# A two-block transformer layer on one core: first projection from the raw input, router logits from the unnormed residual

## What is computed

```python
def rmsnorm(x, g):
    return x * rsqrt(mean(x * x, axis=-1) + EPS) * g

h = rmsnorm(x, attn_pre_norm)                    # block 1
proj = h @ w_in
...
x = x + gt1 * (concat([att, conv]) @ w_out)      # block 2
h2 = rmsnorm(x, g_ffn) * (1 + sc2) + sh2         # modulate
aff = softmax(h2 @ w_router)                     # 16 experts
g, idx = top_k(aff.T, 128)
y = (silu(h2[idx] @ w_gate) * (h2[idx] @ w_up)) @ w_down * g
x = x + gt2 * scatter_add(y, idx)
out = rmsnorm(x, g_final)
```

## Time and profile before

| | |
|---|---|
| median of 3 runs | 2589.52 us (2587.97 to 2590.65) |
| profiled execution | 2590.66 us, span 2588.8 us, mean granted clock 0.975 |
| PE, PEld busy | 2452.7 us (95%), 1918.5 us (74%) |
| DVE, ACT, POOL busy | 1610.7 us (62%), 1254.0 us (48%), 689.7 us (27%) |
| DMA | 384.06 MB, mean 148 GB/s |

### The profile page before, as it was taken

The page is one execution under the profiler, slowest core; times in us unless marked ns, Lnnn a source line. Parts: engine busy times, 40 slices in busy tenths (PEclk is TensorE's granted clock), DMA queues, the critical chain, the costliest instruction groups (busy, mean ns, idle before and its releaser), DMA issues.

```text
span 2588.8 us, 32543 instructions
## 1 busy us (share of the span) xinstructions
PE 2452.7 (95%) x11378; PEld 1918.5 (74%) x11378; DVE 1610.7 (62%) x2439; ACT 1254.0 (48%) x1852; POOL 689.7 (27%) x396
## 2 busy tenths in 40 slices
PE   8999899999999999999999999999997999999996
PEld 5787567777778788777778777765764888888884
DVE  5032887756643367665432635588247999999997
ACT  4121554434543323343433421376344888888886
POOL 1222100113434477334456222121220110111100
PEclk9999999999999999999999999999998999999997
DMA  7100000022222264222223111000138999999996
GB/s 279 49 33 17 34 1 1 1 114 82 82 82 97 97 230 146 80 82 84 95 98 114 66 65 49 33 1 1 67 117 316 402 387 386 397 386 390 396 361 219
DMA packets 86601, 384.06 MB, mean 148 GB/s; under 512 B 7980, under 2 KB 9180, under 8 KB 71520
## 3 DMA queue, kind: packets, MB, share of 16 engines
q1 hardware_dynamic: 81744, 365.25, 37.5%
q0 software_dynamic: 4752, 17.43, 2.5%
HBM read 361.60 MB, written 21.05 MB: 148 GB/s over the span
## 4 chain that ended last, share of the span: by engine, by line
PE 72%; issue 11%; DVE 8%; POOL 4%; ACT 4%; DMA 1%; POOLq 0%; SPq 0%; DVEq 0%; ACTq 0%
PE ps L947 10%; PE ps L949 10%; PE ps L948 10%; PE ps L1299 7%; PE ps L1301 7%; PE ps L1300 7%; POOL w_lo L2667 4%; PE ps L756 3%; PE ps L902 2%; PE ps L826 2%; PE ps L828 2%; PE ps L827 2%; PE ps L748 2%; PE ps L1149 1%; PE ps L770 1%
## 5 line engine op out<-in xcount | busy, mean ns | idle before, releaser
L2667 POOL TENSOR_TENSOR w_lo<-arena,w_hi 128x1024 fp32r<-128x1024 f32 x188 | 462.7, 2462 | 746.4 <-ACT w_hi L1544 742.2
L2543 DVE TENSOR_TENSOR e_lo<-arena,e_hi 128x1024 fp32r<-128x1024 f32 x384 | 454.2, 1221 | 45.4 <-ACT e_hi L1875 34.1
L1875 ACT ACTIVATE e_hi<-arena 128x1024 fp32r<-128x1024 f32 x384 | 404.1, 1062 | 103.1 <-PE ps L1301 103.1
L1544 ACT ACTIVATE w_hi<-arena 128x1024 fp32r<-128x1024 f32 x188 | 198.4, 1055 | 362.9 <-PE ps L949 362.9
L947 PE MATMUL ps<-h_hi,w_hi 128*128 128x512 f32 x848 | 342.6, 404 | 21.4 <-POOL w_lo L2667 11.7
L948 PE MATMUL ps<-h_lo,w_hi 128*128 128x512 f32 x848 | 335.9, 396 | 0.0
L949 PE MATMUL ps<-h_hi,w_lo 128*128 128x512 f32 x848 | 335.9, 396 | 0.0
L947 PEld LDWEIGHTS ps<-h_hi,w_hi 128*128 128x128 f32 x848 | 162.9, 192 | 66.1 <-issue 28.1
L1299 PE MATMUL ps<-e_hi,x_hi 128*128 128x512 f32 x512 | 202.2, 395 | 3.0 <-DVE x_lo L2538 2.6
L1301 PE MATMUL ps<-e_lo,x_hi 128*128 128x512 f32 x512 | 199.5, 390 | 0.0
L1300 PE MATMUL ps<-e_hi,x_lo 128*128 128x512 f32 x512 | 199.3, 389 | 0.0
(11 more groups left out here) (372 smaller groups left out, 5094.4 us busy)
## 6 DMA issues: line engine op xcount, KB each, us to landing
arena<-in_w_up SPq DMA_DIRECT2D x108, 1024.0 KB, 7.0
arena<-in_w_down SPq DMA_DIRECT2D x86, 1024.0 KB, 7.2
arena<-in_w_gate SPq DMA_DIRECT2D x64, 1024.0 KB, 9.4
arena<-in_w_in SPq DMA_DIRECT2D x18, 1024.0 KB, 4.8
arena<-in_w_out SPq DMA_DIRECT2D x16, 1024.0 KB, 4.7
arena<-in_w_ada SPq DMA_DIRECT2D x12, 1024.0 KB, 12.1
arena<-in_w_ada SPq DMA_DIRECT2D x24, 512.0 KB, 6.8
routed_rows<-arena SPq DMA_DIRECT2D x8, 520.0 KB, 2.6
```

The lines of the kernel that those rows point to most:

```text
L1544: act_e.activation(w_hi[:, q, :], slot[c][:, q * D:(q + 1) * D], ACT.Copy).then_inc(s_whi, 1)
L1875: act_e.activation(e_hi[:, (2 * sl + a) % RING, :], slot[sl][:, a * D:(a + 1) * D], ACT.Copy).then_inc(s_ehi, 1)
L2543: v.tensor_tensor(e_lo[:, r, :], slot[sl][:, a * D:(a + 1) * D], e_hi[:, r, :].bitcast(F32), ALU.subtract).then_inc(s_elo, 1)
L2667: gp.tensor_tensor(w_lo[:, q, :], slot[c][:, q * D:(q + 1) * D], w_hi[:, q, :].bitcast(F32), ALU.subtract).then_inc(s_wlo, 1)
```

## The change

It has two parts.

Part A, block 1's first projection. `n_hi` and `n_lo` are now made from the raw input times the gain, without the inverse root, as soon as x arrives, and the value product begins on them, plane by plane, while the squares are still being summed. The inverse root multiplies the results at eviction: per row for the value tiles, and with the spread row `rs0` for the 13 input tiles, whose evictions all move to DVE. The value weights are loaded before x. The modulation steps and the bias turn follow the value product.

Part B, block 2's router. The router weights are scaled by `gsc` (gain times 1 + scale) and multiplied with the residual rows `xT` before the norm; the shift's share (`logits_shift`) is computed once, and DVE multiplies the logits with the inverse root and adds the shift. The products give the logits in rows at once: `first_logits` for the first half, `second_logits(k)` plane by plane for the second, each plane in its own columns, summed by DVE. Row tiles are stored in another order with three buffers, the second half's hT is made by GpSimd and ACT behind the logits, and the gate product is taken apart between row turns and positions.

```diff
-            keep_clock(10)
-            mean(0)
-            pe.wait_ge(s_bias, 16)
-            bias_turned(range(2))
-            spread(0)
-            bias_turned(range(2, 4)).then_inc(s_flip, 1)
+            keep_clock(6)
+            pe.wait_ge(s_n1, 2)
+            for k in range(KT):
+                if k == KT // 2:
+                    pe.wait_ge(s_ilo, 1)
+                pe.wait_ge(s_nhi, k + 1)
+                for u in range(4):
+                    value_product(u // 2, u % 2, k, False)
+                pe.wait_ge(s_h, k + 1)
+                for u in range(4):
+                    m = value_product(u // 2, u % 2, k, True)
...
+            for t in range(2, 4):
+                for h in range(2):
+                    if t == 3:
+                        pe.wait_ge(eva if h else evv, 1)
+                    for k in range(KT):
+                        if (t, h, k) == (2, 1, 2):
+                            mean(0)
+                        if (t, h, k) == (3, 0, 4):
+                            spread(0)
...
             pe.wait_ge(s_rs, 1)
-            modulations(range(4))
+            modulations(range(2))
+            pe.wait_ge(s_bias, 16)
+            bias_turned(range(2, 4))
+            modulations(range(2, 4))
+            bias_turned(range(2)).then_inc(s_flip, 1)
             modulations(range(4, KT))
...
+            v.wait_ge(s_n1, 1)
+            v.tensor_tensor(v_lo[:, 0:KT // 2], wv[:, 0:KT // 2], v_hi[:, 0:KT // 2].bitcast(F32), ALU.subtract).then_inc(s_n1, 1)
+            def first_input_low(ks):
+                for k in ks:
+                    if k < 4:
+                        v.wait_ge(s_nhi, k + 1)
+                    else:
+                        v.wait_ge(s_sq, k + 1)
+                    v.scalar_tensor_tensor(n_lo[k], xT[:, k, :], col("attn_pre", k), n_hi[:, k, :].bitcast(F32), ALU.mult, ALU.subtract).then_inc(s_h, 1)
+            sums(0, {1: lambda: first_input_low(range(3))} | {i: (lambda i=i: first_input_low((i + 1,))) for i in range(2, KT - 1)})
+            diagonal(0)
...
             for t in range(13):
+                for h in range(2):
+                    first_tile(t, h)
                 if t == 5:
                     v.wait_ge(s_mod, 1)
...
                 if t == 3:
                     sums(1)
                     diagonal(1)
...
+            def second_logits(k):
+                pe.wait_ge(eva if k % 2 else evv, T_OUT2 + 4 + k // 2 + 1)
+                if k == 0:
+                    pe.wait_ge(s_rm, 1)
                 for i in range(4):
+                    c = (4 * k + i) * NE
+                    m = pe.matmul(ps[:, 7, c:c + NE], xT[:, k, (4 + i) * P:(5 + i) * P], wr_scaled[:, k, :], start=True, stop=True)
...
-            output_part2(KT + 1, {2: lambda: spread(12)})
-            for i in range(2):
-                output_part2(KT + 2 + i, {1: lambda: row_turn(2 * i), 5: lambda: row_turn(2 * i + 1)})
-            output_part2(KT + 4, {0: lambda: logits(0), 6: lambda: logit_rows(0)})
-            output_part2(KT + 5, {5: lambda: row_turn(4)})
-            output_part2(KT + 6, {1: lambda: row_turn(5), 5: lambda: row_turn(6)})
-            output_part2(KT + 7, {1: lambda: row_turn(7)})
+            output_part2(KT + 1, {2: lambda: spread(12), 4: lambda: first_logits(0), 6: lambda: first_logits(1)})
+            output_part2(KT + 2, {1: lambda: first_logits(2), 4: lambda: first_logits(3)})
+            output_part2(KT + 3, {2: lambda: second_logits(0), 5: lambda: second_logits(1)})
+            output_part2(KT + 4, {2: lambda: second_logits(2), 6: lambda: row_turn(0)})
+            output_part2(KT + 5, {2: lambda: second_logits(3), 6: lambda: row_turn(1)})
+            output_part2(KT + 6, {2: lambda: second_logits(4), 6: lambda: row_turn(2)})
+            output_part2(KT + 7, {3: lambda: row_turn(3)})
+            for k in range(5, KT):
+                second_logits(k)
+            mean(13)
...
+            for k in range(6):
+                row_turn(6 + k)
+                second_gate(k)
+            for j in range(12, 2 * NT):
+                row_turn(j)
...
+            def affinity_shifted(half):
+                part = slice(4 * half, 4 * half + 4)
+                lg = ps[:, 7, 0:4 * NE].rearrange("p (a b) -> p a b", a=4)
+                v.wait_ge(s_lg, half + 1)
+                if half == 0:
+                    vc_.mark(v.tensor_copy(lg_shift, ps[:, 7, 4 * NE:5 * NE]))
+                else:
+                    lg = aff[:, part, :]
+                    vc_.link(v.tensor_reduce(lg.rearrange("p a b -> p (a b)"), ps[:, 7, :].rearrange("p (k c) -> p c k", k=KT), AX_X, ALU.add))
+                vc_.link(v.tensor_tensor(aff[:, part, :], lg, rms[half][:, 0:4].unsqueeze(2).to_broadcast([P, 4, NE]), ALU.mult))
+                vc_.link(v.tensor_tensor(aff[:, part, :], aff[:, part, :], lg_shift.unsqueeze(1).to_broadcast([P, 4, NE]), ALU.add))
...
             def second_gated(k):
                 gated(KT + k)
+                if k == 2:
+                    affinity_shifted(0)
                 if k == 3:
                     affinity(0)
             sums(13, {k: (lambda k=k: second_gated(k)) for k in range(2, KT)})
...
             squares(13, lambda k: xT[:, k, hi], lambda k: gated(KT + k),
-                    {1: lambda: (row_out(0), row_out(1), output2_high(KT + 4)), 2: lambda: (row_out(2), row_out(3), output2_high(KT + 5)),
-                     3: lambda: (logits_copied(0), router_exp(0), output2_high(KT + 6)), 4: lambda: (row_out(4), output2_high(KT + 7)),
-                     5: lambda: (row_out(5), row_out(6)), 6: lambda: row_out(7)})
+                    {1: lambda: output2_high(KT + 4), 2: lambda: output2_high(KT + 5), 3: lambda: (router_exp(0), output2_high(KT + 6)),
+                     5: lambda: (row_out(0), output2_high(KT + 7)), 6: lambda: row_out(1), 7: lambda: row_out(2)})
+            row_out(3)
...
+            gp.wait_ge(s_rs, 14)
+            for k in range(KT):
+                gp.tensor_tensor(hT[:, k, HALF:S], xT[:, k, HALF:S], NORM_AT[13][2], ALU.mult).then_inc(s_hp, 1)
+
+            for b in range(3):
+                gp.wait_ge(s_tkst[b], rows_kept(b))
...
             sp.wait_ge(tps, 2 * (T_OUT2 + 8))
-            expert_weights(0, 0)
-            for j in range(8, 10):
-                store_row(j)
-            sp.wait_ge(s_hb, 5 * KT)
-            for i in range(4):
-                sp.dma_start(slot[8 + i].rearrange("p (a n) -> p a n", a=2), wga[i][:, :, 5 * D:6 * D]).then_inc(wl[8 + i], 16)
-            for j in range(10, 2 * NT):
+            for i in range(1, 4):
+                sp.dma_start(gate2_w[i].rearrange("p (a n) -> p a n", a=2), wga[i][:, :, 5 * D:6 * D]).then_inc(wl[8 + i], 16)
+            for j in range(2):
+                expert_weights(0, 0, None, (2 * j, 2 * j + 1))
+                store_row(4 + 2 * j)
+                store_row(5 + 2 * j)
+            expert_weights(1, 0, None, (3,))
+            for j in range(8, 2 * NT):
                 store_row(j)
```

More of the change, by code:

```diff
@@ L196, in bass_two_blocks @@
         gt2B = view(156, D)
+        gate2_w = [view(192, ITEM), slot[6], slot[10], slot[11]]
         g_fin = view(160, D)
-        silu_b = view3(48, KT, P)
         fin = [view(4 * i, D) for i in range(8)]
@@ L1250, in _, with second_gate @@
             m.then_inc(s_at, 1)
-            for j in range(12, 2 * NT):
-                row_turn(j)
-            pe.wait_ge(s_sb, 1)
-            pe.wait_ge(s_rte, 2 * NT)
-            for k in range(KT):
+            spread(13)
+            def second_gate(k):
+                if k == 0:
+                    pe.wait_ge(s_rs, 14)
+                    pe.wait_ge(s_aff, 3)
                 if k % 2 == 0:
@@ L1391, in _, with first_input_high @@
             act_e.activation(scT[:, :, 1:2], col("cctx", 0, 8), ACT.Silu).then_inc(s_silu, 1)
-            squares(0, lambda k: xT[:, k, :], lambda k: [(xl[k // 2], 16)])
+            act_e.wait_ge(extra, 16)
+            act_e.activation(v_hi[:, 0:KT // 2], wv[:, 0:KT // 2], ACT.Copy).then_inc(s_n1, 1)
+            act_e.activation(v_hi[:, KT // 2:KT], wv[:, KT // 2:KT], ACT.Copy).then_inc(s_ihi, 1)
+            def first_input_high(k):
+                act_e.wait_ge(xl[k // 2], 16)
+                act_e.activation(n_hi[:, k, :], xT[:, k, :], ACT.Copy, scale=col("attn_pre", k)).then_inc(s_nhi, 1)
+            squares(0, lambda k: xT[:, k, :], lambda k: None, {k: (lambda k=k: first_input_high(k)) for k in range(KT)})
             def first_high(n):
@@ L1909, in _ @@
             part_high(3, 1, 1, 0, True)
-            count(5, 6)
+            count(5, 2)
             count(6, 0)
-            for b in range(2):
-                act_e.wait_ge(s_tkst[b], 16 * NT)
+            for b in range(3):
+                act_e.wait_ge(s_tkst[b], rows_kept(b))
             columns(0, 0)
@@ L2014, in _ @@
[L2014 to L2029 removed]
+                at, scale = VALUE_BANK[t], rms[0][:, 2 * t:2 * t + 1]
@@ L2474, in _ @@
```

(16 more changed lines are left out.)

356 lines of the change are left out of this document (168 added, 188 removed).

## The result

The changed kernel takes 2610.29 us (median of 4 runs, 2606.61 to 2613.06) against 2588.74 for the kernel before in the same runs: ratio 1.0075, 95% interval 1.0060 to 1.0091. It is 0.75% slower. The forecast was 2590.1 with a range of 2578 to 2599, so the time lies outside it. The profiled execution has a span of 2608.2 us against 2588.8.

A forecast was written before the change was run, and what follows sets the result against it. TensorE, busy 95% of the span, was taken to bound the kernel. Part A +3.9 and part B -3.3 (6.8 - 11.7 + 1.1 + 0.5) gave +0.6: 2590.1 us on the median's scale, range 2578 to 2599.

The forecast's parts named there:

- Part A: Block 1's first projection: -4.9 to first input tile, +5.1 idle, +3.0 clock, +0.7 last tile; +3.9 us in all.
- loop in k: Value product's start: from k = 4 square, n_lo and add wait on each other, 3.65 us per k; TensorE follows.
- TensorE idle behind tile 3: After input tile 3 TensorE waits for DVE's evictions and a sum held by GpSimd: +5.1 us, lower bound 2.9.
- Part B in the projection: Second half of block 2's output projection: new inserts 25.5 us against 18.7 before, so its last product moves by +6.8.
- the wait at second_logits: Second half's router products in the output projection wait for s_rm: TensorE idles 4.85 us and loses 2.5 of clock behind.
- Part B behind T: After T, the output projection's last product: positions at T + 40.3 instead of T + 52.0 (-11.7 us), gather +1.1.
- The +0.5 for the gt2B add: Behind the output projection: the gt2B add (1.23 us) moves between the first weight splits, +0.5 us (0 to 1.2).
- The removed products: Before the first expert: fillers removed, gate-2 product beside the row path except two steps; forecast to cost or give nothing.
- Rival 1: Row path not last: positions 35.3 us after the output projection (-5.0), gather no slower (-1.1): faster, 2584; chance 0.25.
- Rival 2: TensorE's clock holds through both idles, -5.5 us: faster, 2584.6; chance 0.12.
- Rival 3: Clock drops in the value product's k loop and stays down, +9.3 us: slower, 2599; chance 0.11.
- Rival 4: Behind the output projection GpSimd's multiplies for hT hold up top-k, +4.6 us: slower, 2594.7; chance 0.10.

The follow-up runs named there:

- part B alone: Kernel before with only the router change (logits from unnormed rows, gate 2 between row turns, new store order): 2602.25 us, ratio 1.0051.
- Experiment 3: Changed kernel with small router products spaced out: 2609.13 us; with the second half's in another PSUM bank: 2603.83; with both: 2596.84.
- part A alone: Kernel before with only the first-projection change (raw input, inverse root at the evictions), router as before: 2600.03 us, ratio 1.0035.

## Why the prediction was wrong, step by step

**Part A, +3.9 forecast, +5.1 in the profiled execution, +6.1 over the eight kernels that have it.** The mechanism was right in each step, and the last two figures would be 1.6 more against part B alone's execution instead of before's. First tile 89.8 against 89.83; loop in k 3.65 against 3.55; TensorE idle behind tile 3 5.1 against 5.04; clock behind it 3.0 against 3.2 (the mean of tile 5 is at 168.5, 3.3 late, with -4.96 and 5.04 ahead of it). VectorE's three steps at the last tile were 0.7 against 0.6 (the next TensorE step starts 3.9 late). The term that is missing is the half clock behind that last gap: the step took 3.70 instead of 1.99.

**Part B in the projection, +6.8 forecast, +12.4 measured: the first failed step.** The count of the small products held, and their price wherever the clock was 1.00 (60 x 0.21 = 12.6); the wait at second_logits was 4.56 against 4.85, the clock behind it 3.0 against 2.5, the row turns' waits 1.5 and 0.5 against 1.65 and 0.4. The step "a product with few columns costs 0.21 us at full clock" treated TensorE as busy and therefore at full clock. It was busy, and the clock fell: 16 router products took 5.6 us instead of 3.4 and 13 large ones 0.43 instead of 0.23, together about 5. Experiment 3 shows it, since spacing them alone kept the clock at 1.00. The term at fault is the 12.6 us, which should have carried these 5 us more.

**Part B behind T, -11.7 + 1.1 forecast at the first product, +1.2 measured: the second failed step, and the largest.** The miss is 11.8 us in the profiled pair, and 9 to 12 over the kernels with this code. Top-k was right (T + 8.2 against 8.8, end 34.7 against 35.3). On the row path:

- Stores: rows 4, 6 and 8 landed at T + 22.4, 30.5 and 35.5 where 18.5, 26.0 and 31.1 were forecast. The error is nearly all there by row 4 (3.9 us), and two things account for it. The forecast let each store wait only for what was issued ahead of it, but when row 4 landed the queue had moved 6.9 MB (worked out from its packets), and only 6.0 were row 4 and what stood ahead of it: 0.9 MB issued behind it, 2.2 us at the forecast's 2.5 us per MB. And the first 5 us moved 251 GB/s where the next 15 moved 405, which is 1.9 us; why is not shown.

```profile
1956.20:1961.20 5.00, 4.57 (x27) 4.17 (x27) 3.72 (x13) 4.46 (x8) 0.00 (x0) 0.66 0.83 251
1961.20:1976.20 15.00, 9.91 (x54) 6.39 (x53) 13.99 (x45) 3.10 (x4) 9.87 (x8) 0.94 1.02 405
```

- The last four turns and evictions took 7.7 us (1992.57 to 2000.2) instead of 6, the turns at half clock. With the late stores that put positions at T + 46.5 instead of 40.3.
- The gather waits for the last rows' stores too, and here they come after positions. The prediction wrote that "positions also wait for all 16 row_outs" and then timed the gather from positions, three microseconds on. It started 5.4 us behind positions, at T + 51.9 instead of 43.4.
- "The gather now runs against 5 MB of weights": I gave it 7.5 us, the median of gathers; it took 9.8, and 5.1 without the weights.

Together 8.5 us in the start (6.2 in positions, 2.3 in the wait for the stores), about 2.6 in the transfer and 0.7 in the turn behind it, which ran at half clock: 11.8. The +0.5 for the gt2B add does not show: what the first expert lost is its clock, below.

**The removed products, cost "nothing".** They were the fillers and the gate-2 product that stood ahead of the first expert. In the changed kernel TensorE idles 5.28 us there and enters the expert at 0.50, its 1.2 GHz level, which costs 2.7 us over the first products (0.43 us each until 2025.6, then 0.23). That the missing products are the cause is not shown: five put back held the clock up to the first expert product and it fell behind it, as it did in part A alone, where none had been removed. What decides it there stays open.

**Rivals.** Rival 1 (row path not last) was wrong in the other direction. Rival 2 (the clock holds through both idles) did not come: it was 0.50 behind each. Rival 3 (k loop at half clock) did not come: the clock was 1.00 from 25 us on. Rival 4 (GpSimd's multiplies hold top-k) did not come either. VectorE's maxima beside them in the changed kernel:

```profile
1965.92 0.43 DVE L2556 MAX8 arena<-arena 128x8 f32<-128x256 f32 x1
```

```profile
1963.97 9.87 POOL L2822 TENSOR_TENSOR arena<-arena 128x512 f32<-128x512 f32 x8 [20.99 <-ACT arena L1424]
```

0.43 us each, as before. The Trainium skill's rule (SBUF — State Buffer, Who interferes with whom) holds here, and the term 0 was right. No rival had the clock falling without idle time or the stores later than the sum, and those two made the time.

## What to carry to other kernels

Cost a wait on a chain of engines from the last thing that the consumer waits for, not from the step beside it: the semaphores in front of the gather said stores, and following them would have found 2.3 of the missing 8.5 us. Cost a store on a busy queue with some of what is issued behind it, too. When a change replaces wide matmuls by many narrow ones, keep large ones between them, and give what reads them a bank of its own. And when a queue is to carry stores on the critical path beside weights, place the stores first and leave the weights that the next stage does not need at once for behind it, but check who needs them next.

## What the runs showed that was not expected

**The clock falls without idle time.** In the changed kernel it fell from 1.00 to 0.50, its 1.2 GHz level, while TensorE was busy all the time; the 16 products of 16 columns had begun at 1886.35.

```profile
1886.00:1889.00 3.00, 3.00 (x28) 2.96 (x27) 2.87 (x4) 2.08 (x4) 0.34 (x1) 1.00 0.01 5
1889.00:1899.00 10.00, 10.00 (x37) 8.84 (x37) 0.00 (x0) 0.63 (x1) 0.00 (x0) 0.50 0.00 0
```

The Trainium skill, page TensorE: Matmul & The Clock Gate, section Part 1: The HAM clock gate, ties the clock to how busy TensorE has been; by the profile's busy time it would have stayed up, and the measurement decides: narrow products did not hold it.

**A tie between VectorE and GpSimd.** In block 1's convolution VectorE's add and GpSimd's subtraction start at the same moment. In the changed kernel GpSimd went first, the add took 2.93 us and everything behind it came 1.7 later:

```profile
710.44 2.93 DVE L2226 TENSOR_TENSOR arena<-arena 128x512 f32<-128x512 f32 x1
710.44 2.39 POOL L2736 TENSOR_TENSOR w_lo<-arena,w_hi 128x1024 fp32r<-128x1024 f32 x1 [1.24 <-ACT w_hi L1570]
```

With part B alone, where both start at 703.83, VectorE went first, and it was GpSimd that took longer:

```profile
703.83 0.69 DVE L2197 TENSOR_TENSOR arena<-arena 128x512 f32<-128x512 f32 x1
703.83 2.95 POOL L2707 TENSOR_TENSOR w_lo<-arena,w_hi 128x1024 fp32r<-128x1024 f32 x1 [1.25 <-ACT w_hi L1559]
```

All 14 kernels have the same code at this place, and each execution falls on one side. In six the add takes 2.90 to 2.93 us, and it is 63.5 us from the mean ahead of the convolution to the one behind it; in the other eight GpSimd's subtraction takes 2.93 to 2.97, and it is 61.8 to 61.9. Before lies on the fast side and the changed kernel on the slow one, so 1.6 of the 19.4 us between the two profiled executions come from this tie and not from the change. Such ties are one reason why executions of the same code differ by some microseconds here.
